# Query-rank steps one step later, and modulation pieces fetched in pairs, in a hybrid attention and mixture-of-experts layer

## The reference

```python
mod_lat = (silu(c) @ w_mod + b_mod).reshape(B, 6, 1, D)
mod_ctx = (silu(c_ctx)[None] @ w_mod + b_mod).reshape(1, 6, 1, D)
h  = modulate(rms_norm(x, g_norm1), mod_lat[:, 0], mod_lat[:, 1])
hc = modulate(rms_norm(ctx, g_norm1), mod_ctx[:, 0], mod_ctx[:, 1])
p_lat, p_ctx = h @ w_in, hc @ w_in      # 512 query-rank, 256 + 64 key/value, 3 x 1024 columns
# two attention groups, output projection, gated residual; then
# 16 experts (expert-choice routing, SwiGLU), gated residual
```

## Time and profile before

| | us |
|---|---|
| median of 3 runs | 1990.37 |
| the profiled execution | 1989.72 |
| its span, first to last instruction | 1987.9 |
| PE busy | 1905.2 |
| DVE busy | 866.4 |
| ACT busy | 455.3 |
| POOL busy | 207.2 |

### The profile page before, as it was taken

One profiled execution on the slowest core, in us unless ns is written; L12 is line 12 of the kernel. 1 busy time (PEld: TensorE's weight loads), 2 busy tenths in 40 slices (PEclk: granted clock), 3 DMA queues, 4 the chain that ended last, 5 costly groups with the idle time before them and its releaser, 6 DMA issues.

```text
span 1987.9 us, 26289 instructions
## 1 busy us (share of the span) xinstructions
PE 1905.2 (96%) x10396; PEld 1225.6 (62%) x10396; DVE 866.4 (44%) x1746; ACT 455.3 (23%) x1186; POOL 207.2 (10%) x434
## 2 busy tenths in 40 slices
PE   4999999999999999999999999999989999999998
PEld 2578787888889989888876333535344353534433
DVE  5558878773256666644434140302213031221343
ACT  4233223122156666632222000000000000000000
POOL 0004112011145543100000000000000000000000
PEclk9999999999999999999999999999999999999999
DMA  9967888883122112242269999999999999999998
GB/s 401 421 235 288 327 311 291 278 295 125 57 60 91 46 46 78 111 170 106 106 248 378 410 428 428 431 431 431 431 432 431 429 429 431 431 432 432 430 425 357
DMA packets 69729, 602.29 MB, mean 303 GB/s; under 512 B 6748, under 2 KB 24412, under 8 KB 35176
## 3 DMA queue, kind: packets, MB, share of 16 engines
q1 hardware_dynamic: 56016, 589.01, 72.9%
q10 hardware_dynamic: 13160, 10.03, 1.5%
q0 software_dynamic: 432, 1.57, 0.2%
HBM read 583.80 MB, written 16.79 MB: 302 GB/s over the span
## 4 chain that ended last, share of the span: by engine, by line
PE 59%; DMA 9%; DVE 2%; ACT 1%; issue 1%; ACTq 0%; DVEq 0%
PE SM L1290 9%; PE TM L1290 8%; DMA arena<-in_w_gate_up 7%; PE TM L1333 5%; PE SM L1333 5%; PE TR L1237 2%; PE MJ L1237 2%; PE TM L1042 2%; DMA arena<-in_w_down 2%; PE MJ L917 2%; PE SM L1007 1%; PE SN L1277 1%; PE TN L1046 1%; PE TM L1068 1%; PE SM L1068 1%; PE TM L1070 1%
## 5 line engine op out<-in xcount | busy, mean ns | idle before, releaser
L1290 PE MATMUL SM<-arena 128*64 128x512 f32 x1024 | 250.5, 610 | 26.4 <-DMA arena<-in_w_gate_up 26.4
L1290 PE MATMUL TM<-arena 128*64 128x512 f32 x1024 | 243.1, 594 | 0.0
L1942 DVE SCALAR_TENSOR_TENSOR arena<-arena,csil 128x512 f32<-128x512 f32 x240 | 180.4, 752 | 13.3 <-DMA arena<-in_w_mod 2.4
L1290 PEld LDWEIGHTS SM<-arena 128*64 128x64 f32 x1024 | 71.3, 138 | 162.9 <-issue 161.2
L1290 PEld LDWEIGHTS TM<-arena 128*64 128x64 f32 x1024 | 77.1, 138 | 146.2 <-issue 146.2
L1333 PE MATMUL TM<-arena,cst 128*64 128x512 f32 x512 | 116.9, 598 | 0.7 <-DMA arena<-in_w_down 0.4
L1333 PE MATMUL SM<-arena,cst 128*64 128x512 f32 x512 | 115.4, 597 | 2.0 <-DMA arena<-in_w_down 1.8
L2237 DVE TENSOR_TENSOR brow<-cst,rope_t 128x512 f32<-128x512 f32 x8 | 5.5, 692 | 234.5 <-PE MJ L1263 234.5
L1642 ACT CAST y_hi<-arena 128x512 fp32r<-128x512 f32 x32 | 19.8, 618 | 379.8 <-DVE arena L2282 341.3
L1396 ACT ACTIVATE wh<-wr 128x2048 fp32r<-128x2048 f32 (+1 forms) x32 | 58.7, 1834 | 187.6 <-PE TN L821 141.3
L1851 DVE TENSOR_TENSOR wl<-wr,wh 128x2048 fp32r<-128x2048 f32 (+1 forms) x32 | 70.2, 2193 | 69.6 <-ACT wh L1396 69.6
(11 more groups left out here) (412 smaller groups left out, 3664.8 us busy)
## 6 DMA issues: line engine op xcount, KB each, us to landing
arena<-in_w_gate_up SPq DMA_DIRECT2D x44, 4096.0 KB, 23.4
arena<-in_w_mod SPq DMA_DIRECT2D x96, 1024.0 KB, 6.1
arena<-in_w_gate_up SPq DMA_DIRECT2D x40, 2048.0 KB, 14.2
arena<-in_w_down SPq DMA_DIRECT2D x20, 4096.0 KB, 31.3
arena<-in_w_down SPq DMA_DIRECT2D x24, 2048.0 KB, 28.0
wr<-in_w_na SPq DMA_DIRECT2D x24, 1024.0 KB, 6.9
wor<-in_w_out SPq DMA_DIRECT2D x8, 2048.0 KB, 8.0
xT<-in_tokens_t SPq DMA_DIRECT2D x4, 1536.0 KB, 12.9
```

What stands on the lines that cost most here:

```text
L1290: mm = pe.matmul(GU[b][64 * e:64 * e + CAP, :], xsT[:, k, 64 * e:64 * e + CAP], w[:, 2 * (b // 2) + e, (b % 2) * NB:(b % 2 + 1) * NB], sta ...
L1942: ve.scalar_tensor_tensor(acc, row, c, acc, ALU.mult, ALU.add).then_inc(mod_step, 1)
```

## The change

There are two edits. `MOD_TWOS` names the pieces that are fetched two at a time: a transfer brings pieces n and n+1 (n even), 2 MB, into two neighbouring slots of the ring, 16 KB in each partition. It waits until piece n+1-6 has been used and signals on the semaphore of slot n % 6 alone. The host's layout of `w_mod` follows: a block is stored as two halves with 16 KB in a row, so a single piece is now half of such rows. And each query-rank step is issued one place later: round `pos` runs step k-1 where step k was, and step k where step k+1 was, with k = 2(pos-1). Round 1 has no step between its quarters, and three steps follow the loop instead of two.

```diff
+MOD_TWOS = range(0, 56)
...
+        mod_two = [arena.take((96 + 16 * i) * K, 2 * KQ, NB) for i in range(MOD_RING // 2)]
...
-            return t["w_mod"][block, kq].rearrange("p (k n) -> p k n", n=NB)
+            return t["w_mod"][block, kq // 2][:, kq % 2 * KQ * NB:(kq % 2 + 1) * KQ * NB].rearrange("p (k n) -> p k n", n=NB)
+
+        def mod_signal(n):
+
+            return ma_in[(n - n % 2 if n in MOD_TWOS else n) % MOD_RING]
+
+        def mod_count(n):
+
+            place = (n - n % 2 if n in MOD_TWOS else n) % MOD_RING
+            return 16 * sum(m % MOD_RING == place and not (m in MOD_TWOS and m % 2) for m in range(n + 1))
...
-                    if n >= MOD_RING:
-                        sp.wait_ge(ma_used, n - MOD_RING + 1)
-                    sp.dma_start(mod_a[n % MOD_RING], mod_piece(pos, kq)).then_inc(ma_in[n % MOD_RING], 16)
+                    if n in MOD_TWOS and n % 2:
+                        continue
+                    last = n + 1 if n in MOD_TWOS else n
+                    if last >= MOD_RING:
+                        sp.wait_ge(ma_used, last - MOD_RING + 1)
+                    if n in MOD_TWOS:
+                        sp.dma_start(mod_two[n % MOD_RING // 2], t["w_mod"][pos, kq // 2].rearrange("p (k n) -> p k n", n=NB)).then_inc(ma_in[n % MOD_RING], 16)
+                    else:
+                        sp.dma_start(mod_a[n % MOD_RING], mod_piece(pos, kq)).then_inc(ma_in[n % MOD_RING], 16)
...
-                pe.wait_ge(ma_in[n % MOD_RING], 16 * (n // MOD_RING + 1))
+                pe.wait_ge(mod_signal(n), mod_count(n))
...
                 mod_quarter(pos, 0)
                 mod_quarter(pos, 1)
-                qa_step(k)
+                if k:
+                    qa_step(k - 1)
                 mod_quarter(pos, 2)
                 mod_quarter(pos, 3)
                 if pos + 1 < 2 * MODB:
-                    qa_step(k + 1)
+                    qa_step(k)
                     mod_columns(pos)
                 else:
                     mod_columns(pos)
-                    qa_step(k + 1)
-            qa_step(KD - 2)
-            qa_step(KD - 1)
+                    qa_step(k)
+            for k in range(KD - 3, KD):
+                qa_step(k)
...
-        "w_mod": to_rows(w_mod.reshape(D, 6 * MODB, NB).swapaxes(0, 1), 6 * MODB, 4),
+        "w_mod": to_rows(w_mod.reshape(D, 6 * MODB, NB).swapaxes(0, 1), 6 * MODB, 2),
```

## The result

The changed kernel took 1993.99 us in the median of 15 runs (1992.83 to 1998.02), the kernel before 1990.71 us (1989.74 to 1992.24) beside it. The ratio is 1.0018, with a 95% interval of 1.0011 to 1.0024: slower by 3.3 us, clear of noise, and inside what the text above called no change (0.2%). The forecast was 1991.7. The profiled execution took 1995.53 us, its span 1993.7.

What follows compares the result with a forecast made beforehand. It took PE as the bound (busy 1905.2 of 1987.9 us), transfers near their limit too. Last column turn 1.5 us earlier, then 12.26 us instead of 9.41: 1.3 us later, giving 1991.7 us, range 1988.4 to 1994.4.

Steps and rivals of the forecast that it cites:

- The waits on h_lo go, and transfers are late next: Modulation rounds: PE's seven waits on DVE's h_lo (6.1 us) vanish, but PE then waits for transfers and can't keep that.
- The rate of the pairs: 2 MB transfers move 427 GB/s against 421, worth 1.1 us; last pair lands at 109.4 us, key/value weights at 111.0.
- Rival C: Larger packets bring nothing and only the order counts: +2.4 us, 1992.8 us; chance 0.20.
- B: Rival: the DMA queue runs dry between pairs in rounds 2 to 7, 6 us over the forecast, 1998 us; chance 0.08.
- Step 11 at about 110.1: Round 7: with pair 14 landed at 104.5 us, PE ends query-rank step 11 at about 110.1 us.
- So nothing shows: DVE's low part of weights 2 and 3, 1.9 + 2.3 us with the copy, hides behind PE's 1.85 + 2.90 us.
- 12.26 with four: From last column turn to first key/value matmul: 12.26 us with four query-rank steps, against 9.41 with three.
- The sum: Last column turn 1.5 us earlier (114.65 us), first key/value matmul 1.3 us later (126.9 against 125.58).
- kv after 129 us: Sign that the forecast is wrong: first key/value matmul (kv) starting before 124.5 or after 129 us.
- Carried to the end: Behind the first key/value matmul, later stages including the expert stream start later by the same amount.
- Rival A: The six rounds shrink to PE's own 10.37 us: matmul 2.8 us earlier, 1987.6 us; chance 0.10 with its partial forms.
- Rival D: Strided pieces of `load_mod` land late (15 us instead of 5.1), holding DVE in the next stage: 1996 us; chance 0.04.

Runs made afterwards that it cites:

- e3: The changed kernel with query-rank step 12 moved ahead of the last column turn, into PE's 2.02 us wait: 1989.83 us, ratio 0.9996.
- e4: The changed kernel with seven unused matmuls in each of PE's two long waits (round 3, ahead of the last column turn): 1992.03 us, ratio 1.0006.
- e1: The later steps only, with the 1 MB transfers and layout of the kernel before: 1994.41 us, ratio 1.0016.
- e5: The changed kernel with DVE's last copy of the sums ahead of the low part of the key/value weight: 1990.98 us, ratio 1.0002.
- e7_longer_wait: The kernel before with two more unused DVE copies, lengthening PE's wait ahead of the last column turn: 1992.98 us, ratio 1.0013.
- e8: The kernel before with two more unused DVE copies lengthening PE's last wait, and eight unused matmuls filling it: 1991.37 us, ratio 1.0006.

## Why the prediction was right in its range and wrong in its size

- *The waits on h_lo go, and transfers are late next*: right. 6.1 us of waits became 4.5 us of waits for pieces.
- *The rate of the pairs*: right. 426 GB/s in 40 to 80 us against 421; the last pair landed at 109.4 us and the key/value weights at 111.0, as forecast, and the order-only kernel, with the old transfers, had the weights at 112.0. Rival C is out as to the rate, but no time came of the rate that can be seen (the pairs alone: 1.0001). B is out: the DMA share was 0.99 to 1.01 in every ten us from 30 to 100. In 105 to 110 us it was 0.78 against 0.96 before, so the sign "DMA share still 1.0 to 109 us" failed; the traffic ended about 1 us earlier. The traffic of 40 to 80 us, and line L654 at 99 us, in the kernel after:

```profile
DMA packets 1313, 17.05 MB, mean 426 GB/s; under 512 B 144, under 2 KB 144, under 8 KB 144
```

```profile
L654 SPq DMA_DIRECT2D wr<-in_w_kv x1: 432/432/432, 99.2 to 99.2; - x1
...
DMA to landing us min/median/max: 11.8/11.8/11.8
```

- *Step 11 at about 110.1*: wrong. The pair for round 3 was waited for (1.79 us), which was in the plan, but the quarters behind it ran at half clock, 1.63 us more. PE had no wait left between 69 and 112 us to make that up, so step 11 ended at 112.09. It, not the weights, released ACT's high part, and the last turn came at 116.03, not 114.65: 1.4 us. With round 3 at full clock step 11 ended at 111.16 (e3) and 111.23 (e4), and e4 had the turn at 115.18. So 0.9 us is the low clock, and 0.5 us is there without it: the sum let the landing of pair 14 set step 11, but in e3 PE's last wait for a piece ended at 85.05 us, and its own work set it from there. ACT and DVE in the kernel after, which answer to the earlier trace rows:

```profile
112.58 1.27 ACT L1414 ACTIVATE wh<-wr 128x1280 fp32r<-128x1280 f32 x1 [0.54 <-PE TM L838]
```

```profile
113.89 1.49 DVE L1869 TENSOR_TENSOR wl<-wr,wh 128x1280 fp32r<-128x1280 f32 x1 [1.32 <-ACT wh L1414]
115.29 0.68 DVE L1855 COPY arena<-TN 128x512 f32<-128x512 f32 x1
```

- *"So nothing shows"*, of DVE's low part of the weights 2 and 3: wrong by little. In the changed kernel the turns of blocks 3 and 5 come 0.77 us behind the last matmul's start instead of 0.46, behind DVE's copy of the sums, which stands behind that low part (for block 3 it ended at 74.47 us, the turn is at 74.53).
- *"12.26 with four"*, from the last turn to kv: wrong, 13.53. The wait ahead of the turn was forecast (behind DVE's wl, where it stood), its price was not: step 12 took 4.42 us at half clock instead of 2.89. In e4 this term is 11.93, so the clock took 1.6 us, and the term itself was 0.3 us too long.
- *The sum*: 1.3 us forecast, 4.0 measured; 1.4 and 1.3 are what the two terms above were off by. By cause it is 0.85 us for the low clock in round 3, 1.6 for the low clock behind the last turn, and 1.5 for the order by itself. By the test that the prediction set itself (kv after 129 us) it is wrong. That the time lies in its range is partly luck: the upper end, 1994.4, was drawn for small losses of rival B, which didn't come, and 1993.99 is just under it. The step that failed is the treatment of a PE wait as costing its length only: the clock behind the waits stood in no term.
- *Carried to the end*: right, 3.98 us at 129 us and 4.04 at 1073 us.
- *Rival A*: out; no ten us from 30 to 110 moved over 431 GB/s. Rounds 4 to 6 did take only 10.6 us each (turns at 74.53 and 106.37) without a wait, presumably because pieces had come in while PE was at half clock; that wasn't tested. *Rival D*: out; `load_mod`'s pieces landed in 5.2 us in the median against 5.1, and PE was busy 320.44 us in 127 to 450 us in both kernels.
- *The rules on size*: from 1 MB to 2 MB transfers in a full queue the rate went from 421 to 426 GB/s. The Trainium skill (*DMA: Bandwidth & Descriptors*, "Measured (HBM→SBUF, 128 partitions, SWDGE, issued from GpSimd)") has 341 GB/s at 1 MB, which no row here shows; the fixed cost per packet of its section "Why small descriptors are slow (HBM only)" would give 0.6%, an estimate from that page and half of the measured 1.2%.

What stays open is which wait brings the low clock. Among PE's unfilled waits from 38 us to kv, in the traces of all the kernels here, each of the seven from 1.79 us up had a stretch at 0.50 behind it. Of four between 1.38 and 1.68 us, one had (1.41 in e1) and three had not (1.38 in the changed kernel, 1.43 in e1, 1.68 in e5). Up to 1.13 us none had, the waits of 0.8 to 1.0 us in the kernel before among them, except 0.60 us in the changed kernel and 0.61 us in e5, both in round 1 at the end of a stretch with many waits, where e3 had full clock behind 0.62. Length alone doesn't decide, and the place can differ for the same instructions.

## What to carry to other kernels

Where a transfer stream sets the pace, moving work out of one wait of the matmul engine mostly makes another longer: PE's waits from 38 us to kv sum to 7.3 us before and to 6.5 us in the changed kernel. But a few long waits cost more than many short ones, because the granted clock halved behind each wait of 1.79 us or more. So spread independent work to keep each wait short, above all ahead of a stretch that has no slack behind it, and read the granted clock by 1 us windows around each wait over 1 us. And count what stands behind the last arrival: a step pushed there is paid in full.

## What the runs showed of the hardware

A stretch at 0.50 granted clock cost PE 1.4 to 1.6 us (1.63 in round 3, 1.37 in e7_longer_wait), and twice as much in e1_late_only, behind a wait of 2.63 us: 15.14 us from turn to kv against 11.93 at full clock. Work whose results nobody reads prevented it ahead of the last turn (e4, and e8 against e7). It need not begin at once: behind the last turn the clock fell after PE had been busy again for over a us (117.7 us, the turn at 116.03). The Trainium skill (*TensorE: Matmul & The Clock Gate*, "HAM oscillation — how this bites in real kernels") names waits on DMA between bursts of matmuls as what brings the half clock on. The trace agrees for the wait on DMA of 1.79 us, shorter than the 3 to 5 us of that section's example, and here a wait on DVE of 2.0 us did it as well.
